# Once per head of the attention, the steps that normalise its output come ahead of rotations, conversions and low halves

## The reference

```python
    def block(args):
        q_blk, start = args
        sc = jnp.einsum("bhiqd,bhikd->bhiqk", q_blk, kt).astype(jnp.float32) * scale
        ...
        pr = jax.nn.softmax(jnp.where(mask, sc, -jnp.inf), axis=-1)
        attn = pr[:, :, 0] - lam * pr[:, :, 1]
        return jnp.einsum("bhqk,bhkv->bhqv", attn.astype(vt.dtype), vt)
    ...
    o = rms_norm(o, subln_g) * (1.0 - lambda_init)
    return o.reshape(bsz, s, h * 2 * d)
```

## Time and profile before

| | us |
|---|---|
| median of 3 runs | 2474.03 (2471.67 to 2475.98) |
| the profiled execution | 2473.14 |
| its span, first to last instruction | 2471.4 |

### The profile page before, as it was taken

How to read it: one execution, slowest core, us unless ns; L and a number is a source line. 1 busy time by engine, 2 the same in 40 slices (tenths; PEclk the granted TensorE clock), 3 DMA queues, 4 the chain that set the end, 5 groups by cost and what they waited for, 6 DMA issues and landing times.

```text
span 2471.4 us, 32150 instructions
## 1 busy us (share of the span) xinstructions
PE 2355.5 (95%) x11866; PEld 1938.3 (78%) x11866; DVE 1401.8 (57%) x2047; ACT 1001.0 (41%) x1864; POOL 1104.1 (45%) x825
## 2 busy tenths in 40 slices
PE   7899998999999989999988999999999998999997
PEld 6677887887777868888866778988777787788886
DVE  6767675546664558777867665631666533422323
ACT  2355454245554232322334555542555432422322
POOL 1445544443444434444433655454344444444452
PEclk9999999999999989999989999999999999999998
DMA  6211123622222425455422112233221232222321
GB/s 237 77 60 60 52 69 120 205 93 69 69 68 68 172 96 206 171 196 188 161 95 74 54 55 66 69 98 99 69 68 61 75 121 93 78 94 95 102 94 51
DMA packets 84812, 250.27 MB, mean 101 GB/s; under 512 B 7472, under 2 KB 34480, under 8 KB 79280
## 3 DMA queue, kind: packets, MB, share of 16 engines
q1 hardware_dynamic: 84656, 248.22, 30.0%
HBM read 244.00 MB, written 4.19 MB: 100 GB/s over the span
## 4 chain that ended last, share of the span: by engine, by line
issue 37%; PE 27%; POOL 16%; POOLq 14%; DVE 4%; DMA 1%; ACT 1%; DVEq 1%; ACTq 1%; SPq 0%
POOL w_lo L1755 15%; POOLq L1757 14%; PE gemm L553 4%; PE gemm L555 4%; PE gemm L554 4%; PE aux L714 3%; PE gemm L576 2%; PE gemm L577 2%; PE gemm L578 2%; PE aux L618 1%; PE aux L701 1%; PE aux L725 1%; PE aux L730 1%; POOL smalls L1743 1%; PE aux L605 1%
## 5 line engine op out<-in xcount | busy, mean ns | idle before, releaser
L1755 POOL TENSOR_TENSOR w_lo<-raw,w_hi 128x512 fp32r<-128x512 f32 x704 | 978.7, 1411 | 1265.0 <-ACT w_hi L903 1257.6
L903 ACT ACTIVATE w_hi<-raw 128x1024 fp32r<-128x1024 f32 x352 | 371.1, 1057 | 689.5 <-PE gemm L555 620.8
L553 PE MATMUL gemm<-h_hi,w_hi 128*128 128x512 f32 x1504 | 607.2, 404 | 25.1 <-DVE conv L1414 19.7
L555 PE MATMUL gemm<-h_hi,w_lo 128*128 128x512 f32 x1504 | 592.5, 394 | 0.0
L554 PE MATMUL gemm<-h_lo,w_hi 128*128 128x512 f32 x1504 | 592.4, 394 | 0.0
L553 PEld LDWEIGHTS gemm<-h_hi,w_hi 128*128 128x128 f32 x1504 | 287.0, 191 | 86.4 <-issue 30.1
L555 PEld LDWEIGHTS gemm<-h_hi,w_lo 128*128 128x128 f32 x1504 | 286.3, 190 | 62.2
L554 PEld LDWEIGHTS gemm<-h_lo,w_hi 128*128 128x128 f32 x1504 | 287.2, 191 | 58.7 <-issue 1.9
L553 PE MATMUL gemm<-op_hi,w_hi 128*128 128x512 f32 x608 | 238.5, 392 | 0.2
L555 PE MATMUL gemm<-op_hi,w_lo 128*128 128x512 f32 x608 | 236.8, 389 | 0.0
L554 PE MATMUL gemm<-op_lo,w_hi 128*128 128x512 f32 x608 | 236.6, 389 | 0.0
(11 more groups left out here) (195 smaller groups left out, 3451.3 us busy)
## 6 DMA issues: line engine op xcount, KB each, us to landing
raw<-stream SPq DMA_DIRECT2D x336, 512.0 KB
ada_late<-stream SPq DMA_DIRECT2D x30, 1024.0 KB, 4.8
ada_early<-stream SPq DMA_DIRECT2D x40, 256.0 KB, 4.0
raw<-stream SPq DMA_DIRECT2D x32, 256.0 KB
ada_pe<-stream SPq DMA_DIRECT2D x4, 1024.0 KB, 16.3
ada_first<-stream SPq DMA_DIRECT2D x4, 1024.0 KB, 18.3
x<-xT SPq DMA_DIRECT2D x2, 2048.0 KB, 10.9
xsave<-x SPq DMA_DIRECT2D x1, 2048.0 KB, 7.3
```

The costliest lines, as they stand in the source:

```text
L553: mm(o, w_hi[:, slot, k, cols], hi[:, k, :], start=k == 0, stop=False)
L555: last = mm(o, w_lo[:, slot, k, cols], hi[:, k, :], start=False, stop=k == KB - 1)
L903: A(w_hi[:, slot, ks], raw[:, slot, ks], ACT.Copy).then_inc(hi_ready, 1)
L1755: gp.tensor_tensor(w_lo[:, slot, ks], raw[:, slot, ks], w_hi[:, slot, ks].bitcast(F32), ALU.subtract)
```

## The change

In the ticks with n % 4 == 1 (from tick 5 on) four calls move. ScalarE's `o_square` goes ahead of `taken`; VectorE's `o_mean` goes ahead of `difference`, and `o_norm` ahead of the rotations and gates; GpSimd's `rsqrt_of_o` goes ahead of `low`. No instruction is added or removed.

```diff
@@ ScalarE @@
-                    taken(T_ATT + n)
                     if n > TB and n % TB == 1:
                         o_square(n // TB - 1)
+                    taken(T_ATT + n)
                     for half in HALVES_AT[T_ATT + n]:
                         convert(l, half // 2, half % 2)
@@ VectorE @@
+                    if n > TB and n % TB == 1:
+                        o_mean(n // TB - 1)
                     difference(n)
                     if n > TB and n % TB == 1:
-                        o_mean(n // TB - 1)
+                        o_norm(n // TB - 1)
                     for j in range(2):
                         for m in since(T_ATT + n, U_AT, U_AO, 1 + j):
...
-                    if n > TB and n % TB == 1:
-                        o_norm(n // TB - 1)
@@ GpSimd @@
                 for n in range(len(ATT)):
+                    if n > TB and n % TB == 1:
+                        rsqrt_of_o(n // TB - 1)
                     for part in HALVES_AT[T_ATT + n]:
                         low(l, part // 2, part % 2)
-                    if n > TB and n % TB == 1:
-                        rsqrt_of_o(n // TB - 1)
```

## The result

| | median, us | runs |
|---|---|---|
| before | 2474.84 (2471.67 to 2475.98) | 4 |
| changed | 2454.62 (2452.64 to 2456.45) | 4 |
| ratio | 0.9922, 95% interval 0.9909 to 0.9935 | |

Faster by 0.8%; 2455.3 us had been forecast. The profiled execution has a span of 2450.8 us against 2471.4.

A forecast was written before the change was run, and what follows sets the result against it. TensorE, busy 95% of the span, was taken as the bound, so only its idle or slow-clock time could be saved. -13.7 + 1.8 - 6.8 = -18.7 us from the 2474.03 us median gave 2455.3 us, range 2448.5 to 2465.5.

The forecast's parts named there:

- The chain from swap to squares to low half to root: Tick 5: swap delays ScalarE's squares, low half delays GpSimd's root, so the norm is late; 4.2 us from mean to root.
- The waits: TensorE's L815 waiting for VectorE's output norm in 12 places, 16.2 us shown; their removal was forecast at -13.7 us.
- The new stall: Scores behind six rotation ticks start late because ScalarE's exponentials move back: at most 0.32 us each, +1.8 us taken.
- The conversion: ScalarE in ticks 5, 13 and 21: starts 5.8 us after the scores instead of 5.4, 0.46 us later.
- The clock: TensorE's four half-clock stretches behind long waits vanish: 4 x 1.7 = -6.8 us.
- The sum: Whole kernel: waits, late scores and half clock together, -13.7 + 1.8 - 6.8 = -18.7 us.
- The first: Rival on TensorE's clock: the four drops have another cause and remain, only -11.9 us, 2462.1 us; chance 0.24.
- The second: Rival at L815: TensorE waited for something other than the norm, nothing gained, 2475.8 us; chance 0.06.
- The third: Rival at the key swap's second half: it waits behind VectorE's norm, shifting ScalarE 2.7 or 4.9 us, 2482.1 us; chance 0.04.

The follow-up runs named there:

- root_only: Kernel before with only GpSimd's part of the change, the root ahead of the low half: 2450.45 us against 2471.76, ratio 0.9915.
- square_only: Kernel before with only ScalarE's part of the change, the squares ahead of the swap: ratio 1.0008.
- square_back: Changed kernel with ScalarE's part undone, swap first and then the squares: 2455.66 us, ratio 0.9933.
- root_x4: Changed kernel with GpSimd's root done four times over for heads 0 to 6, same result: 2462.71 us, ratio 0.9962.
- root_back: Changed kernel with GpSimd's part undone, low half first and then the root: 2473.35 us against 2471.76, ratio 1.0005.

## Why the prediction was right

**The wait and its cause.** The chain from swap to squares to low half to root was read rightly, and root_only shows that its last link alone mattered. The waits were sized at 13.7 us. By the same measure, from turning to fill, the 12 places took 30.05 us before against 15.89 now, 14.2 less; 0.5 of it is half clock inside one of them. So 13.7. One reading in it is inexact: the 4.2 us from the mean's end to the root's start hold none of the root's own work; to its end it is 5.2 us (576.32 to 581.54), of which 1.0 is work.

**The new stall.** Forecast 1.8 us, measured 2.6: the scores are 0.45 us late in each of six ticks, less the 0.13 that tick 13 already had. The conversion moved as forecast, from 5.37 to 5.81 us after the scores. The term was mis-sized behind it: the exponentials begin 578.35 - 577.26 = 1.09 us after the conversion where it had been 0.96 (576.26 to 577.22), which I had carried over. No run here shows why it grew.

**The clock.** Forecast 6.8 us. The four drops are gone, and at the 1.6 us that one costs in this trace they are worth 6.4. That drops belong to the waits is no luck of one execution, as the table above shows. That there were just four of them is chance: six waits of nearly the same length in square_only had a drop each.

**The sum.** -13.7 + 2.6 - 6.4 = -17.5 us; the stretch shows -17.6. The forecast of -18.7 is 1.1 us too large by the terms, while the medians fell by 20.2 us, 2.6 more than the stretch. That the time came out within 0.7 us of the forecast is partly luck: those 2.6 us are in no term of the prediction and are not explained here.

**The rivals.** The first (the clock does not come back) fell with the drops. The second (the norm was not what TensorE waited for) fell with root_only, where nothing but its timing changed. The third (ScalarE becomes the bound) fell too: the swap began at 574.85, ahead of the norm at 576.15, and the exponentials moved by 0.57 us (from 6.33 to 6.90 us after the scores) and not by 2.7 or 4.9. What I had not seen was a fourth: VectorE's later steps as the next to be late. In the full change they hold. In square_back and root_x4, with the squares 2.0 us or the root 3.5 us later, they already cost 0.8 and 1.1 us behind each rotation.

**What I gave the change credit for.** I costed three parts together and let each stand. Costed one by one, the trace of before would have shown that with the root alone moved the norm ends near 9.1 us, just ahead of TensorE at 9.3, and that ScalarE's part brings nothing but a stall.

## What to carry to other kernels

When a tiny instruction is late, look at what stands ahead of it in its own engine's queue before moving anything upstream: here 1 us of work behind 3 us of work that nobody needed for three ticks was the whole gain, and moving its producers earlier took 2.6 us of it back (by the stretch; the medians do not tell it). Move one engine at a time, since a step put ahead of others delays all of them, and the delay shows up at another instruction, one or two ticks later. And price a wait on TensorE with the half clock behind it: here 1.6 us per stretch, on top of waits hardly longer than that, and less where the slower clock hides another late step.

## What the hardware showed

- Waits of 1.4 to 2.3 us between dense matmuls were followed by 3.4 us at 1.2 GHz in 19 of 32 cases, waits of 2.5 to 3.6 us in 20 of 20, and the 14 waits up to 0.7 us never. In 4 of the 39 cases it was 6.8 us, and in some it began inside the wait. The same wait in the same place had it in one layer and not in another.
- Small VectorE instructions took longer beside a GpSimd subtraction: L1608 (one element per partition) took 0.86 us and L1609 1.53 us there (square_back), against 0.16 and 0.42 beside an idle GpSimd (root_only). L1608 ended at 587.80, right behind the first subtraction of the low half (586.49 to 587.78). In the kernel before, L1617 did the same in tick 9 of layer 1: 1815.13 to 1816.41, 1.28 us instead of 0.17, beside a subtraction from 1815.10 to 1816.39. So in these two cases (L1608 and L1617) the small instruction ended with the subtraction beside it.
- The other way round there is a cost too: the two subtractions of a low half took 2.50 us (root_back, tick 5) where VectorE did no rotation beside them, and 2.96 us where it did.
